# Delta rule: triangular inverses built to 32 wide on quarter tiles of the array, then joined block by block

## What is computed

```
gam = jnp.cumsum(gc, axis=-1)
decay = jnp.where(incl, jnp.exp(jnp.where(incl, diff, 0.0)), 0.0)
a_mat = jnp.where(strict, bc[..., :, None] * jnp.einsum('...id,...jd->...ij', kc, kc) * decay, 0.0)
tinv = lax.linalg.triangular_solve(eye + a_mat, jnp.broadcast_to(eye, a_mat.shape),
                                   left_side=True, lower=True)
value = tinv @ (vc * bc[..., None])
kcum = tinv @ (kc * (bc * jnp.exp(gam))[..., None])
...
def step(s, xs):
    val, kcm, qkm, qd, kd, gl = xs
    u = val - kcm @ s
    o = qd @ s + qkm @ u
    s = s * gl + jnp.swapaxes(kd, -1, -2) @ u
    return s, o
```

## Time and profile before

| | us |
|---|---|
| median of 3 runs (2347.85 to 2354.05) | 2351.05 |
| the profiled execution | 2350.54 |
| its span | 2348.9 |
| stage of the delta rule, in the profile | 536 |
| one pair, first p of level 2 to the first p of the next pair (1247.57 to 1285.83) | 38.3 |

### The profile page before, as it was taken

The page is one execution under the profiler, slowest core; times in us unless marked ns, Lnnn a source line. Parts: engine busy times, 40 slices in busy tenths (PEclk is TensorE's granted clock), DMA queues, the critical chain, the costliest instruction groups (busy, mean ns, idle before and its releaser), DMA issues. The chain is left out here.

```text
span 2348.9 us, 37740 instructions
## 1 busy us (share of the span) xinstructions
PE 2250.2 (96%) x14798; PEld 1685.9 (72%) x14798; DVE 1074.3 (46%) x2075; ACT 581.6 (25%) x1340; POOL 1103.3 (47%) x982
## 2 busy tenths in 40 slices
PE   9897999899999999999999999999999999999997
PEld 7675555477777777677777777686876767777776
DVE  5343675435421341477886556453643154313322
ACT  2003676410000000255564234232420010000011
POOL 3212555357653564565656232422426365644653
PEclk9999999999999999999999999999999999999999
DMA  9734002822212212312221030301203112112211
GB/s 328 217 96 161 1 2 73 292 72 70 74 72 84 79 54 78 134 56 73 74 75 39 6 109 7 108 2 38 78 24 130 72 72 84 60 72 97 83 72 41
DMA packets 55883, 197.16 MB, mean 84 GB/s; under 512 B 15458, under 2 KB 29538, under 8 KB 39714
## 3 DMA queue, kind: packets, MB, share of 16 engines
q1 hardware_dynamic: 49186, 177.52, 21.6%
q0 software_dynamic: 3088, 14.03, 1.8%
q10 hardware_dynamic: 3440, 3.25, 0.4%
HBM read 170.86 MB, written 32.17 MB: 86 GB/s over the span
## 5 line engine op out<-in xcount | busy, mean ns | idle before, releaser
L2018 PE MATMUL ps<-xn,ring 128*128 128x288 f32 x768 | 198.8, 407 | 5.4 <-DVE xn L2121 3.2
L2018 PE MATMUL ps<-hid,ring 128*128 128x288 f32 x768 | 192.8, 406 | 0.0
L2018 PEld LDWEIGHTS ps<-xn,ring 128*128 128x128 f32 x768 | 145.3, 190 | 48.3 <-DVE xn L2121 5.9
L2018 PEld LDWEIGHTS ps<-hid,ring 128*128 128x128 f32 x768 | 145.6, 190 | 40.6 <-ACT p L2055 0.7
L2101 POOL TENSOR_TENSOR prod<-prod,rstd 128x1152 f32<-128x1152 f32 x32 | 84.0, 2624 | 179.5 <-DVE prod L2185 163.2
L2055 ACT ACTIVATE p<-ps 128x288 f32<-128x288 f32 x48 | 19.8, 412 | 597.4 <-PE ps L2018 597.4
L3430 PE MATMUL ps<-xn,ring 128*128 128x288 f32 x512 | 137.1, 414 | 3.6 <-PE ps L3499 3.6
L1122 POOL TENSOR_SCALAR ring<-ring,fac 128x128 f32<-128x128 f32 (+2 forms) x96 | 92.5, 979 | 88.4 <-DVE fac L1555 88.4
L2018 PE MATMUL ps<-x_sum,wsum 128*128 128x288 f32 x512 | 130.6, 407 | 3.4 <-DVE x_sum L2125 1.9
L2075 POOL TENSOR_TENSOR wsum<-ring 128x512 f32<-128x512 f32 x64 | 82.0, 1281 | 99.5 <-DMA ring<-in_w_mlp 91.6
L2018 PE MATMUL ps<-hid_sum,wsum 128*128 128x288 f32 x512 | 128.4, 407 | 0.2
(11 more groups left out here) (530 smaller groups left out, 4939.1 us busy)
## 6 DMA issues: line engine op xcount, KB each, us to landing
ring<-in_w_mlp SPq DMA_DIRECT2D x64, 1024.0 KB, 4.8
ring<-in_w_gdn_in SPq DMA_DIRECT2D x16, 1024.0 KB, 4.8
ring<-in_w_nsa_in SPq DMA_DIRECT2D x9, 1024.0 KB, 18.0
ring<-in_w_gdn_z SPq DMA_DIRECT2D x8, 1024.0 KB, 4.9
x<-in_seq_state SPq DMA_DIRECT2D x4, 2048.0 KB, 8.9
out_seq_state<-x SPq DMA_DIRECT2D x4, 2048.0 KB, 10.9
ring<-in_w_gdn_out SPq DMA_DIRECT2D x8, 1024.0 KB, 5.6
out_win_old<-in_win_rows POOLq DMA_DIRECT2D x1, 8064.0 KB, 46.6
```

The costliest lines, as they stand in the source:

```text
L2018: mm = nc.tensor.matmul(S.ps[:, base + BANK[p], 0:HT], stationary(p, blk.units[pair // 4], pair % 4), moving(blk.kind, p, pair), start=pai ...
```

## The change

- `LEVELS` loses the level 32. At the levels that are left, t, tt and u are held as four heads x 32 columns, the four diagonal blocks of 32 below one another on the partitions. A product is 32 x 32, one for each head and each of the four diagonal quarters of the array: 16 for a tile in each of p and the two halves of q, where there were 8 of 64 x 64.
- t and tt stand side by side in the same tile, and the two products of q in the same PSUM bank, so one addition of 128 x 256 on DVE does both sums. u is 128 x 128.
- Blocks of 32 are joined to 64 by block products: p32 (8 products of 32 x 32 for a tile), u32 (DVE), q32 (12 products), then a copy on DVE (t10) and copies on ACT. Then p64, u64, q64 join 64 to 128 as before, with operands from a tile in which the blocks of 64 are put together.
- ACT has, for a tile, two copies of t and four copies of tt after level 16 (32 partitions x 128 elements each), two copies of q32's result from PSUM, and the last copy of 64 x 256 as before. Three zero corners are set once, and one more on POOL for each tile.
- The first weighing on DVE is four operations of 32 x 128 for a tile, not two of 64 x 256. POOL's masks work on 128 elements, not 256.
- In the pass of Q the products are 32 x 32 as well, also in kcum (two of 32 rows for a head) and in the value product.

On PE, one level and the end of the inverses of the first pair. In the names, L3311, L3322 and L3328 are p and the halves of q, L3335 and L3340 are p64 and q64, and L3346 is kcum.

The diff, cut to its core:

```
-    i, j = i % 64, j[:, 0:64]
-    for b in (2, 4, 8, 16, 32):
+    i, j = i % 32, j[:, 0:32]
+    for b in (2, 4, 8, 16):
...
-LEVELS = (2, 4, 8, 16, 32)
+LEVELS = (2, 4, 8, 16)
...
+def compact(t, rows, at=0):
+    return t[0:rows].rearrange("p j t -> p (j t)")[:, at:at + 128].rearrange("p (j t) -> p j t", j=4)
+
+
+def quarters(rows):
+    return [slice(32 * q, 32 * q + 32) for q in range(rows // 32)]
...
                     for j in range(4):
-                        for r in range(blocks):
-                            mm = nc.tensor.matmul(to(0, j, r), a(j, r, r), part(t, j, r), start=True, stop=True)
+                        for r in quarters(rows):
+                            mm = nc.tensor.matmul(to(0, j, r), a(j, r, r), t[r, j, :], start=True, stop=True)
...
+                    if not (c is Q and n == 1):
+                        for j in range(4):
+                            for r in quarters(rows):
+                                nc.tensor.matmul(to(2, j, r), tt[r, j, :], u[r, j, :], start=True, stop=True)
                     for j in range(4):
-                        for r in range(blocks):
-                            mm = nc.tensor.matmul(to(2, j, r), part(u if n else first_u(b, rows), j, r), part(tt, j, r),
-                                                  start=True, stop=True)
+                        for r in quarters(rows):
+                            mm = nc.tensor.matmul(to(2, j, r, 128), u[r, j, :], tt[r, j, :], start=True, stop=True)
...
+                    wait_step(pe, c, "vec", job, "i16")
                     for j in range(4):
-                        mm = nc.tensor.matmul(to(0, j, 1), a(j, 0, 1), part(t, j, 0), start=True, stop=True)
+                        for r in (0, 2):
+                            mm = nc.tensor.matmul(to(0, j, q4[r + 1]), a(j, q4[r], q4[r + 1]), t[q4[r], j, :], start=True, stop=True)
...
+                    wait_step(pe, c, "vec", job, "u32")
+                    for j in range(4):
+                        nc.tensor.matmul(to(2, j, q4[1]), tt[q4[1], j, :], u[q4[1], j, :], start=True, stop=True)
+                        for r in (0, 2):
+                            mm = nc.tensor.matmul(to(2, j, q4[r], 128), u[q4[r + 1], j, :], tt[q4[r + 1], j, :], start=True, stop=True)
...
+                    wait_step(pe, c, "vec", job, "t10")
+                    wait_step(pe, c, "act", job, "td1")
+                    wait_step(pe, c, "pool", job, "corner")
...
                     wait_step(pe, c, "vec", job, "u64")
+                    wait_step(pe, c, "act", job, "mid1")
...
             def tile_end(c, b, job):
                 B = buf[b]
-                wait_step(act, c, "vec", job, "it32")
-                for r in range(2):
-                    h = slice(64 * r, 64 * r + 64)
-                    done(a_.activation(inverse[h, b, :, h], turned(b, 128)[h], ACT.Copy), c, "act")
+                q4 = quarters(128)
+                wait_step(act, c, "vec", job, "i16")
+                for q in range(2):
+                    done(a_.activation(quarter64(b, q4[q])[:, :, q4[q]], compact(B["t"], 128)[q4[q]], ACT.Copy), c, "act")
+                for q in q4:
+                    done(a_.activation(inverse[q, b, :, q], turned(b, 128)[q], ACT.Copy), c, "act")
+                yield
+                wait_step(act, c, "pe", job, "q32")
+                for q in (0, 2):
+                    done(a_.activation(inverse[q4[q], b, :, q4[q + 1]], S.ps[q4[q], 4 * b + 2, 128:256].rearrange("p (j t) -> p j t", j=4), ACT.Copy), c, "act")
+                yield
...
                         ends = [tile_end(c, b, job) for c, b, i, job in jobs(hg, pr)]
-                        for _ in range(2):
+                        for _ in range(4):
...
-                        h = slice(0, 64 if lv == LEVELS[-1] else rows)
-                        done(v.tensor_tensor(t[h], t[h], bank(0, 256)[h], ALU.add), c, "vec")
-                    done(v.tensor_tensor(tt, tt, bank(2), ALU.add), c, "vec")
+                        done(v.tensor_tensor(both, both, S.ps[0:rows, 4 * b + 2, 0:256], ALU.add), c, "vec")
```

More of the change, by code:

```diff
@@ L3000, in tile_steps @@
     pe = ["vturn", "kk", "diff", "upto_row", "turned"]
-    vec = ["w0"] + ([] if seq else ["w1"]) + ["a0", "a1", "a2", "a3"]
+    vec = ["w0", "w1"] + ([] if seq else ["w2", "w3"]) + ["a0", "a1", "a2", "a3"]
     for n, b in enumerate(levels):
         pe += [f"p{b}", f"q{b}"]
-        vec += [f"u{b}"] + (["qk0"] if n == 0 else []) + ([] if seq and b == levels[-1] else [f"i{b}"]) + [f"it{b}"]
-    pe += ["kcum", "value", "out", "state"] if seq else ["p64", "q64", "kcum", "value", "state_read", "state", "out"]
-    vec += ["u"] if seq else ["u64", "u", "state0", "state1", "state2", "state3"]
-    act = ["vb", "decay", "upto", "kdec", "kb"] + ([] if seq else ["first", "high", "low"]) + ["kcum"]
-    return {"pe": pe, "vec": vec, "act": act, "pool": ["g_rows", "pair", "pair_i", "t", "tt", "qk", "qdec"]}
+        vec += [f"u{b}"] + (["qk0"] if n == 0 else []) + [f"i{b}"]
+    pe += ["kcum", "value", "out", "state"] if seq else ["p32", "q32", "p64", "q64", "kcum", "value", "state_read", "state", "out"]
+    vec += ["u"] if seq else ["u32", "t10", "u64", "u", "state0", "state1", "state2", "state3"]
+    act = ["vb", "decay", "upto", "kdec", "kb"] + ([] if seq else ["td0", "td1", "d0", "d1", "d2", "d3", "mid0", "mid1", "low"]) + ["kcum"]
+    return {"pe": pe, "vec": vec, "act": act, "pool": ["g_rows", "pair", "pair_i", "t", "tt", "qk"] + ([] if seq else ["corner"]) + ["qdec"]}
 NORM_STEPS = {"pe": ["out_turned"], "vec": ["square_sum", "mean", "rstd", "normed"], "act": ["square", "root", "out"]}
@@ L3172, in first_inverse @@
                 out = compact(buf[b]["t"], rows) if name == "t" else turned(b, rows)
-                done(g.tensor_tensor(out, pair(b, rows), S.c(mask)[0:rows].unsqueeze(1).broadcast_to([rows, 4, 64]), ALU.mult),
+                done(g.tensor_tensor(out, pair(b, rows), S.c(mask)[0:rows].unsqueeze(1).broadcast_to([rows, 4, 32]), ALU.mult),
                      c, "pool")
@@ L3316, in tile_front @@
                         wait_step(pe, c, "pool", job, "tt")
-                    else:
-                        wait_step(pe, c, "vec", job, f"it{levels[n - 1]}")
-                    if not (c is Q and n == 1):
-                        for j in range(4):
-                            for r in range(1 if lv == LEVELS[-1] else blocks):
-                                nc.tensor.matmul(to(0, j, r, 256), part(tt, j, r), part(u if n else first_u(b, rows), j, r), start=True, stop=True)
                     if n == 0:
@@ L3338, in tile_front @@
                     wait_step(pe, c, "vec", job, "u64")
+                    wait_step(pe, c, "act", job, "mid1")
+                    pe.wait_ge(corner_zero, 3)
                     for j in range(4):
-                        mm = nc.tensor.matmul(to(2, j, 0), part(u, j, 1), part(tt, j, 1), start=True, stop=True)
+                        mm = nc.tensor.matmul(S.ps[low, 4 * b + 2, 256 + 64 * j:320 + 64 * j], quarter64(b, high)[:, j, :], inverse[high, b, j, high],
+                                              start=True, stop=True)
                     done(mm, c, "pe")
@@ L3350, in tile_front @@
                     wait_step(pe, c, "act", job, "kb")
-                    wait_step(pe, c, "vec", job, f"it{levels[-1]}")
+                    wait_step(pe, c, "vec", job, f"i{levels[-1]}")
                     for j in range(4):
-                        mm = nc.tensor.matmul(S.ps[:, 4 * b + 3, 64 * j:64 * j + 64], B["kb"][0:64, j, :], part(tt, j, 0),
-                                              start=True, stop=True)
+                        for r in quarters(TS):
+                            mm = nc.tensor.matmul(S.ps[:, 4 * b + 2 + r.start // 32, 32 * j:32 * j + 32], B["kb"][r, j, :], tt[r, j, :],
+                                                  start=True, stop=True)
                     done(mm, c, "pe")
@@ L3481, in _ @@
                     mm.then_inc(zm_used, 1)
-                    mm = nc.tensor.matmul(S.ps[0:TS, 1, cols], turned(0, TS)[:, j, :], B["vb"][0:TS, j, :], start=False,
-                                          stop=True, skip_group_check=True)
+                    for r in quarters(TS):
+                        mm = nc.tensor.matmul(S.ps[r, 1, cols], turned(0, TS)[r, j, :], B["vb"][r, j, :], start=False,
+                                              stop=True, skip_group_check=True)
                 done(mm, Q, "pe")
@@ L3642, in pair_weights @@
                 wait_step(dve, prev, "pe", pj)
-                for r in range(blocks_of(c)):
-                    h = slice(64 * r, 64 * r + 64)
+                for h in quarters(rows):
                     kk = S.ps[h, 4 * b + 2, 0:2 * rows].rearrange("p (a t) -> p a t", a=2)[:, :, h].unsqueeze(2)
```

66 lines of the change are left out of this document (42 added, 24 removed).

## The result

The changed kernel takes 2421.43 us (median of 4 runs, 2415.31 to 2424.33), the kernel before 2350.98: ratio 1.0294, 95% interval 1.0278 to 1.0309, slower by 70 us. The profiled execution is the fastest of the four, 2415.31, with a span of 2413.7, so the two profiles stand 64.8 us apart.

What follows compares the result with a forecast made beforehand. A pair was taken as bound by PE's groups plus DVE's turns. The sum was 2350.5 + 27 (instruction supply and weighing) - 4.5 (pass of Q) + 32 (clock) = 2405 us, range 2345 to 2440.

Steps and rivals of the forecast that it cites:

- the two causes named: PE's instructions arriving too slowly in the pairs' levels, and PE's granted clock falling to 0.50; together given chance 0.48.
- the wide part: Wide products behind the tail, 10.2 us of PE work: 3.4 to 6.8 us at half pace, taken as +2.5 a pair.
- Supply of instructions: Levels 2 to 16: 374 records on hand, the other 1,162 at 71 per us; 18.6 us against 15.56, +3.0 a pair.
- my case with none on hand: Bound for levels 2 to 16 if PE starts with no instructions on hand: 21.6 us, +6.1 a pair.
- The clock: PE's clock falls to 0.50 in the changed pair, slowing tail and wide products: +4.0 a pair, +32 in all.
- The tail without the clock: After level 16 to the last kcum: ACT's sixteen copies in line, 6.8 us for 7.49; a packet's wait makes it 0.
- The joint sum: DVE's addition in the levels: one of 0.42 us in place of two.
- the weighing: First weighing on DVE: four operations a tile at 0.28 to 0.31 us each in place of two, +0.35 a pair.
- Q: Pass of Q: one addition fewer and others on half the elements, -1.1 us a pass, -4.5 for four.
- D: Rival for the levels: narrow products cost as much as wide ones, 29 ns a record; 2410 us, chance 0.05.
- Rival A: Change works as intended: packets come ahead of need and the clock stays; 2315 us, chance 0.17.
- rival C: No supply limit, but the clock falls in levels, tail and wide part: +2.1 a pair, 2363 us, chance 0.08.

Runs made afterwards that it cites:

- e9: Changed kernel with the products p of the pairs' levels issued twice, 512 records a level for 384: 2474.35 us.
- e8: Changed kernel with transposed inverses made by block transpositions on DVE in place of PE's second half of q, 256 records a level: 2362.46 us.
- e3: Changed kernel with an unused 256-column filler product behind each p and q of levels 4 to 16, to hold the clock up: 2427.91 us.
- e1: Kernel before with each 64 x 64 product of the pairs' levels split into two of 32 columns, 384 records a level: 2507.46 us.
- e2: Changed kernel with one 64-column product for each two of 32 columns in levels 2 to 16, 192 records a level: 2339.69 us.

## Why the prediction was right

The kernel is slower by 70 us where I had said 54, for the two causes named. The number is nearer than its terms: the levels were priced at +3.0 a pair and took +6.7, the wide part at +2.5 and took +0.2, and two errors in the tail cancel.

- **Supply of instructions.** Right in mechanism and rate. The packets come 3.5 us apart with waits inside lists, and 72 records per us at the margin (e9) against 71 predicted. The term was +3.0 a pair and measured +6.7. The step that failed is the start of the levels. I let the 374 records on hand be used in 2.3 us at the free pace, and the packets come at 71 per us from then on. The stock itself was about right. Taking the records that PE issued up to its first stop inside a list, less 249 for each packet that came in between, it was 230 to 453 in the eight pairs, 339 in the mean. But PE took longer for them, since level 2 has waits of its own (1.10 us on DVE's L3701 among them), and the next packet came late. In the first pair of round 3:

```profile
1542.07:1547.01 4.94, 3.22 (x210) 2.70 (x209) 4.23 (x12) 4.24 (x12) 3.52 (x6) 0.90 0.78 323
```

After these 4.9 us, some 419 records, PE stops for 2.10 us. The next packet starts 4.5 us after the first p and is used 2.5 us later. In the mean of the pairs the first stop ends 6.5 us after the first p, with 432 records issued, where my sum has them after 3.1 us. The other 1,104 take 15.7 us, 70 per us. So 3.4 of the missing 3.6 us were lost up to that first stop. e8 misses its 12 us by about the same. In three of the eight pairs a data load delays packets, which the earlier trace rows had shown and which I used for the latency only. That the levels come near the 21.6 of my case with none on hand is chance.
- **The clock.** Right that it falls to 0.50, from level 4 on. The term was +4.0 a pair, +1.5 in the tail and +2.5 in the wide part. The tail's was too small: 2.3 to 3.2 us by the one pair of e3. The wide part's failed: I took the fall to last 3.4 to 6.8 us into the wide products, but the clock was back between 0.5 us before and 1.6 us after the first value product, and the wide part took +0.2. Together, by this estimate, 2.5 to 3.4 a pair.
- **The tail without the clock.** I had 6.8 us with ACT's sixteen copies in one row, 4.8 us, as the chain, up to the last kcum product. Up to the value product, as in the table, that is 7.8 (1308.88 and 1309.88 before), and 8.5 with the packet's wait. The copies took 307 ns from SBUF and 268 from PSUM, close to the estimate. But at a clock of 1.00 the tail takes 6.39 us (the pair of e3 above), where ACT starts its copies with the sum of the first tile, 1.4 us before the tail begins. In the changed kernel kcum's products at half pace end it. So I had the tail too long without the clock and the clock's cost in it too small. That +1.5 forecast and +1.7 measured agree is luck.
- **DVE.** The joint sum at 421 ns, the mask at 291 and the weighing at 286 ns an operation came as priced. The +0.35 of the weighing came out as +0.1 in the second pairs.
- **Q.** -1.5 a pass against -1.1.
- **D and the quarters.** A narrow record took 9 ns at 2.4 GHz (29 records of L3330 between 1249.76 and 1250.01) and 13 at 1.2 (28 of L3330 between 1255.34 and 1255.72), not the 29 of D. On tiles of 64 x 64 a record with 32 columns did take 29 ns (e1). The Trainium skill, "TensorE: Matmul & The Clock Gate", section Wait — 56ns, not 53.3ns?, puts its 25 ns for narrow products without regard to the tile; by these runs it is near the truth for 64 x 64 and three times too high for 32 x 32 on four quarters.
- **Rival A.** Its sign was right: with the supply out of the way (e2), the kernel takes 2340, 12 below before by the ratio. I had 2315 for it, with the clock up: the levels came nearly as priced (13.3 with 2.1 of waits left, 12.0 predicted), but the clock is still at 0.50 for 7.4 us of the tail's 9.8. With 2.3 to 3.4 us less in each tail, by the one at a clock of 1.00, it would be 2312 to 2321, an estimate; no run has both limits out of the way. The Trainium skill, "Runtime: NRT & Kernel Launch", section Instruction fetch mechanics, calls the cost of a block mostly hidden; that holds in the kernel before, at 55 records per us, but for 2.2 us of waits in all, and not where PE asks for more than some 70.
- **A slip in rival C.** Its clock costs of 3.4 and 4.0 make 7.4, where I added 5.9; by its own parts it was 2375.

By the table the sum is 53.9 (predicted 24) + 13.8 (12, clock) + 1.6 (20) + 0.4 (3) - 6.1 (-4.5).

## What to carry to other kernels

Splitting products into more and smaller ones can cost more than it saves even if each is as fast as hoped: here PE got about 70 instruction records per us over stretches longer than what it has on hand, and a float32 product is four of them. Count the instructions of a stretch and divide, before counting columns. One pause in the trace that no engine explains, within a list of equal products, was enough to read that rate from, but not how long the records on hand would last; and what is saved on another engine behind such a limit is worth nothing (the joint sum). PE with such stops was also granted half the clock, and that cost the most where it worked without stops again, in the tail. In the kernel before, which had no such limit, taking a third of the levels' products off PE, onto DVE, gained 15 us, and 26 with Q's part.

## What was not expected of the hardware

- A change between products on 32 x 32 and on 64 x 64 tiles costs PE about 0.18 us at 2.4 GHz and some 0.25 at 1.2: alternating them took the time from 2351 to 3201 us, nearly all of the stage at 1.2 GHz, and grouping the same instructions brought it back to 2457.
- On tiles of 64 x 64 a matmul record with 32 columns takes the 29 ns of one with 64; on quarter tiles of 32 x 32 one with 32 columns takes 9 ns at 2.4 GHz and 13 at 1.2.
- A transposition by blocks of 32 x 32 on DVE takes as long as a sum of the same shape (0.34 to 0.36 us from start to start for 128 x 256).
- Instruction packets wait behind data: with 433 GB/s of other transfers PE stood for 4.01 us, with a quiet DMA 1.5.
- In e1 the granted clock stayed at 0.50 from 1410 to 1440 us while PE had records all the time. It had fallen at 1409, after one stop of 2.0 us that ended at 1407.2.
